# From the fourth feed-forward step on, both parts of the scaled tokens as one 512-column matmul operand

## What is computed

```python
h = h + merged @ w_out
hid = causal_dwconv(rms_norm(h, ffn_norm_g) @ w_ffn_up, ffn_conv_w, ffn_conv_b)   # width 3, 2*2816 channels
g_ff, up = jnp.split(hid, 2, axis=-1)
return h + (jax.nn.silu(g_ff) * up) @ w_ffn_down
# the whole is followed by a final RMSNorm
```

## Time and profile before

| | |
|---|---|
| median of 3 runs | 704.9 us (704.57 to 705.47) |
| the profiled execution, its own time | 704.42 us |
| its span, first to last instruction | 702.6 us |
| TensorE busy | 691.7 us, 98% of the span |
| VectorE busy | 493.6 us, 70% |
| ScalarE busy | 372.7 us, 53% |
| mean granted TensorE clock | 0.997 |

### The profile page before, as it was taken

The page is one execution under the profiler, slowest core; times in us unless marked ns, Lnnn a source line. Parts: engine busy times, 40 slices in busy tenths (PEclk is TensorE's granted clock), DMA queues, the critical chain, the costliest instruction groups (busy, mean ns, idle before and its releaser), DMA issues.

```text
span 702.6 us, 13155 instructions
## 1 busy us (share of the span) xinstructions
PE 691.7 (98%) x5210; PEld 657.5 (94%) x5210; DVE 493.6 (70%) x632; ACT 372.7 (53%) x472; POOL 9.7 (1%) x23
## 2 busy tenths in 40 slices
PE   9999999999999999999999999999999999999995
PEld 5999999999999999999999999999899999999994
DVE  5876989697876656667644456665568777777795
ACT  6539776767564554454533333333365555555552
POOL 0000000000100000000000000000000000000001
PEclk9999999999999999999999999999999999999998
DMA  8768576669536345345365755556626655555521
GB/s 236 226 204 278 167 248 178 229 191 355 156 109 190 122 153 180 120 142 159 121 188 182 257 186 156 185 177 222 213 75 206 198 179 179 179 186 188 198 87 60
DMA packets 112192, 127.60 MB, mean 182 GB/s; under 512 B 5358, under 2 KB 101151, under 8 KB 111647
## 3 DMA queue, kind: packets, MB, share of 16 engines
q1 hardware_dynamic: 112159, 127.14, 56.1%
HBM read 126.03 MB, written 2.67 MB: 183 GB/s over the span
## 4 chain that ended last, share of the span: by engine, by line
PE 88%; DVE 6%; ACT 2%; DMA 2%; issue 2%; SPq 0%; POOL 0%; DVEq 0%; POOLq 0%; ACTq 0%
PE ps L358 27%; PE ps L359 27%; PE ps L360 27%; DVE w_lo L330 2%; DVE conv_a L1311 1%; PE ps L400 1%; DMA acs_d<-acs_row 1%; PE ps L668 1%; DMA acs_b<-acs_d 1%; ACT decay L990 1%; PE ps L406 1%; PE ps L704 0%; PE ps L688 0%; DVE tok_lo L1216 0%; PE ps L653 0%
## 5 line engine op out<-in xcount | busy, mean ns | idle before, releaser
L358 PE MATMUL ps<-tok_hi,w_hi 128*128 128x256 f32 x1056 | 301.5, 285 | 1.1 <-DVE w_lo L1220 0.5
L359 PE MATMUL ps<-tok_lo,w_hi 128*128 128x256 f32 x1056 | 298.7, 283 | 0.0
L360 PE MATMUL ps<-tok_hi,w_lo 128*128 128x256 f32 x1056 | 298.7, 283 | 0.0
L330 DVE TENSOR_TENSOR w_lo<-w_raw,w_hi 128x2048 fp32r<-128x2048 f32 x108 | 247.0, 2288 | 67.0 <-ACT w_hi L326 67.0
L326 ACT ACTIVATE w_hi<-w_raw 128x2048 fp32r<-128x2048 f32 x108 | 206.2, 1910 | 57.4 <-PE ps L360 52.5
L358 PEld LDWEIGHTS ps<-tok_hi,w_hi 128*128 128x128 f32 x1056 | 202.4, 192 | 4.0 <-issue 2.0
L359 PEld LDWEIGHTS ps<-tok_lo,w_hi 128*128 128x128 f32 x1056 | 202.5, 192 | 0.4
L360 PEld LDWEIGHTS ps<-tok_hi,w_lo 128*128 128x128 f32 x1056 | 202.5, 192 | 0.0
L358 PE MATMUL ps<-os_hi,w_hi 128*128 128x256 f32 x128 | 36.3, 284 | 0.0
L360 PE MATMUL ps<-os_hi,w_lo 128*128 128x256 f32 x128 | 36.2, 283 | 0.0
L359 PE MATMUL ps<-os_lo,w_hi 128*128 128x256 f32 x128 | 36.2, 283 | 0.0
(11 more groups left out here) (280 smaller groups left out, 1063.8 us busy)
## 6 DMA issues: line engine op xcount, KB each, us to landing
w_raw<-w_in SPq DMA_DIRECT2D x94, 512.0 KB, 4.8
w_raw<-w_ffn_up SPq DMA_DIRECT2D x44, 512.0 KB, 4.4
w_raw<-w_ffn_down SPq DMA_DIRECT2D x22, 512.0 KB, 4.2
w_raw<-w_mem_kv SPq DMA_DIRECT2D x16, 512.0 KB, 4.4
w_raw<-w_br_ssm SPq DMA_DIRECT2D x16, 512.0 KB, 4.4
acs_b<-acs_d SPq DMA_DIRECT2D x4, 1024.0 KB, 6.6
w_raw<-w_br_attn SPq DMA_DIRECT2D x8, 512.0 KB, 4.4
w_raw<-w_br_mem SPq DMA_DIRECT2D x8, 512.0 KB, 4.0
```

Source lines behind the costliest of these rows:

```text
L330: dve.tensor_tensor(w_lo[:, s, :], w_raw[:, s, :], w_hi[:, s, :].bitcast(F32), ALU.subtract).then_inc(lo_ready[s], 1)
L358: pe.matmul(o, a[0], b[0], start=start, stop=False, **kw)
L359: pe.matmul(o, a[0], b[1], start=False, stop=False, **kw)
L360: return pe.matmul(o, a[1], b[0], start=False, stop=stop, **kw)
```

## The change

From step 3 on the up-projection takes other tokens. They are already scaled: h times gain times the token's factor, with high and low part side by side in one tile, `normed[:, k, 0, :]` and `normed[:, k, 1, :]`. The high part of the weights then meets both in one matmul of 512 columns, which fills a whole bank: the left half gets high times high, the right half high times low. The low part of the weights times the high tokens, 256 columns, is added to the right half. A product now fills two banks (a pair), one for each group of 128 output channels, and its result is the sum of a bank's halves. ScalarE copies the right halves of both banks into the pad (a new instruction that waits for the product), and VectorE adds the left halves to it and frees the pair.

The scaled tokens are made in steps 1 and 2, two quarters in each: VectorE adds the two token parts and multiplies by `rstd_b` (`normalise`), ScalarE makes the high part, VectorE the low part (`normalise_low`). These two steps are written out instead of looped. Some semaphores are merged as well (left out here); that changes no instruction's place.

```diff
+    def gemm_pair(pe, r, s, pair, freed):
+        pe.wait_ge(lo_ready[s], r + 2)
+        pe.wait_ge(bank_free[pair], freed)
+        for j in range(2):
+            b = 2 * pair + j
+            for k in range(KT):
+                w = slice(k * CW + j * P, k * CW + (j + 1) * P)
+                pe.matmul(ps[:, b, :], w_hi[:, s, w], normed[:, k, :, :].rearrange("p a t -> p (a t)"), start=k == 0,
+                          stop=False, skip_group_check=True)
+                mm = pe.matmul(ps[:, b, T:2 * T], w_lo[:, s, w], normed[:, k, 0, :], start=False, stop=k == KT - 1,
+                               skip_group_check=True)
+        mm.then_inc(gemm_done[s], 1)
...
-            with pe.Fori(1, F_STEPS - 2) as f:
+            for f in (1, 2):
                 r = f + (RG - 1)
                 gemm_cols(pe, r, 0, tok_hi, tok_lo)
                 gemm_cols(pe, r, 1, tok_hi, tok_lo)
                 down(r, 2, f, hid_hi, hid_lo)
...
+            with pe.Fori(3, F_STEPS - 2) as f:
+                r = f + (RG - 1)
+                gemm_pair(pe, r, 0, 0, r + 1)
+                gemm_pair(pe, r, 1, 1, r + 1)
+                down(r, 2, f, hid_hi, hid_lo)
+            gemm_pair(pe, RL - 1, 0, 0, RL)
+            gemm_pair(pe, RL - 1, 1, 1, RL)
+            gemm_pair(pe, RL - 1, 2, 0, RL + 1)
+            gemm_pair(pe, RL, 0, 1, RL + 1)
...
     (ScalarE, in ffn)
+                    if len(source) > 2:
+                        s, done = source[2:]
+                        act.wait_ge(gemm_done[s], done)
+                        act.wait_ge(f_step, 8 * f - 4 + 4 * n)
+                        act.activation(pad[:, :, FTAPS - 1:], ps[:, 2 * b:2 * b + 2, T:2 * T],
+                                       ACT.Copy).then_inc(crossed, 1)
...
+                    for q in norm if n == 0 else ():
+                        act.wait_ge(normed_t, 2 * q + 2)
+                        act.activation(normed[:, 2 * q:2 * q + 2, 0, :], norm_t[:, 2 * q:2 * q + 2, :],
+                                       ACT.Copy).then_inc(normed_hi, 1)
...
     (VectorE)
+            def normalise(q):
+                two = slice(2 * q, 2 * q + 2)
+                dve.tensor_tensor(norm_t[:, two, :], tok_hi[:, two, :].bitcast(F32), tok_lo[:, two, :].bitcast(F32),
+                                  ALU.add).then_inc(normed_t, 1)
+                dve.wait_ge(normed_t, 2 * q + 1)
+                dve.tensor_tensor(norm_t[:, two, :], norm_t[:, two, :], rstd_b[:].unsqueeze(1).to_broadcast([P, 2, T]),
+                                  ALU.mult).then_inc(normed_t, 1)
+            def normalise_low(q):
+                two = slice(2 * q, 2 * q + 2)
+                dve.wait_ge(normed_hi, q + 1)
+                dve.tensor_tensor(normed[:, two, 1, :], norm_t[:, two, :], normed[:, two, 0, :].bitcast(F32),
+                                  ALU.subtract).then_inc(normed_lo, 1)
...
+                    else:
+                        dve.wait_ge(crossed, 2 * f + n - 5)
+                        dve.tensor_tensor(inner, ps[:, 2 * b:2 * b + 2, 0:T], inner, ALU.add).then_inc(bank_free[b], 1)
```

More of the change, by code:

```diff
@@ L216, in build @@
     rstd_b = place("rstd_b", R + 18.5, [T])
+    normed = place("normed", R + 56, [KT, 2, T], F32R)
+    norm_t = place("norm_t", R + 72, [KT, T])
     pad_g = place("pad_g", R + 0, [2, FTAPS - 1 + T])
@@ L1147, in _, with ffn @@
             split_hi(act, RG, 0)
[L1150 to L1153, removed]
+            def ffn(f, gate, up, after_gate, after_up, last, first=False, hi=hid_hi, norm=()):
+                for n, (source, pad, conv, tile) in enumerate(((gate, pad_g, conv_g, 0), (up, pad_u, conv_u, FT))):
+                    b, freed = source[:2]
+                    if len(source) > 2:
[4 more added lines that the diff above has]
+                                       ACT.Copy).then_inc(crossed, 1)
+                    act.wait_ge(bank_free[b], freed)
                     if not first:
@@ L1171, in ffn @@
                     split_hi(act, rr, ss)
-            ffn(0, 1, RF + 3, 2, RF + 3, [(RG, 1)], [(RG, 2)], [], first=True)
-            with act.Fori(1, F_STEPS - 2) as f:
+            ffn(0, (1, RF + 3), (2, RF + 3), [(RG, 1)], [(RG, 2)], [], first=True)
+            for f in (1, 2):
                 r = f + (RG - 1)
-                ffn(f, 0, r + 2, 1, r + 2, [(r + 1, 0)], [(r + 1, 1)], [(r + 1, 2)])
-            ffn(F_STEPS - 2, 0, RL + 1, 1, RL + 1, [(RL, 0)], [(RL, 1)], [], hi=last_hi)
-            ffn(F_STEPS - 1, 2, RF + 4, 0, RL + 2, [(RL, 2)], [(RL + 1, 0)], [], hi=end_hi)
+                ffn(f, (0, r + 2), (1, r + 2), [(r + 1, 0)], [(r + 1, 1)], [(r + 1, 2)], norm=(2 * f - 2, 2 * f - 1))
+            with act.Fori(3, F_STEPS - 2) as f:
+                r = f + (RG - 1)
+                ffn(f, (0, r + 2, 0, r + 1), (1, r + 2, 1, r + 1), [(r + 1, 0)], [(r + 1, 1)], [(r + 1, 2)])
+            ffn(F_STEPS - 2, (0, RL + 1, 0, RL), (1, RL + 1, 1, RL), [(RL, 0)], [(RL, 1)], [], hi=last_hi)
+            ffn(F_STEPS - 1, (0, RL + 2, 2, RL), (1, RL + 2, 0, RL + 1), [(RL, 2)], [(RL + 1, 0)], [], hi=end_hi)
             for n in range(2 * NT):
@@ L1571, in _ @@
             dve.memset(pad_u[:, :, 0:FTAPS - 1], 0.0).then_inc(pads_zero, 1)
-            dve.wait_ge(x_again, 16)
+            dve.wait_ge(x_in[0], 32)
             split_lo(dve, RF + 1, 0)
@@ L1587, in _, with ffn, pad_with @@
             dve.wait_ge(pads_zero, 2)
[L1590 to L1595, removed]
+            def normalise(q):
[10 more added lines that the diff above has]
+                                  ALU.subtract).then_inc(normed_lo, 1)
+            def ffn(f, gate, up, early, after_gate, after_up, hi=hid_hi, lo=hid_lo, norm=()):
+                def pad_with(n, pad, splits):
+                    b, s, r = (gate, up)[n][:3]
+                    inner = pad[:, :, FTAPS - 1:]
+                    if len((gate, up)[n]) == 3:
+                        dve.wait_ge(gemm_done[s], r + 1)
+                        dve.tensor_tensor(inner, halves(s), rstd_b[:].unsqueeze(1).to_broadcast([P, 2, T]),
+                                          ALU.mult).then_inc(bank_free[s], 1)
+                    else:
+                        dve.wait_ge(crossed, 2 * f + n - 5)
+                        dve.tensor_tensor(inner, ps[:, 2 * b:2 * b + 2, 0:T], inner, ALU.add).then_inc(bank_free[b], 1)
                     for rr, ss in splits:
@@ L1609, in convolve @@
                                                      ALU.mult, ALU.add).then_inc(f_step, 1)
-                pad_with(sa, ra, pad_g, early)
+                for q in norm:
+                    normalise(q)
+                pad_with(0, pad_g, early)
                 convolve(0, pad_g, conv_g, 0)
-                pad_with(sb, rb, pad_u, [])
+                for q in norm:
+                    normalise_low(q)
+                pad_with(1, pad_u, [])
                 dve.wait_ge(g_tanh, f + 1)
@@ L1625, in ffn @@
                 dve.tensor_tensor(lo[:], hid[:], hi[:].bitcast(F32), ALU.subtract).then_inc(hid_lo_s, 1)
-            ffn(0, 1, RF + 1, 2, RF + 1, [(RG, 0)], [(RG, 1)], [])
-            with dve.Fori(1, F_STEPS - 2) as f:
+            ffn(0, (1, 1, RF + 1), (2, 2, RF + 1), [(RG, 0)], [(RG, 1)], [])
+            for f in (1, 2):
                 r = f + (RG - 1)
-                ffn(f, 0, r, 1, r, [(r, 2)], [(r + 1, 0)], [(r + 1, 1)])
-            ffn(F_STEPS - 2, 0, RL - 1, 1, RL - 1, [(RL - 1, 2)], [(RL, 0)], [(RL, 1)], last_hi, last_lo)
-            ffn(F_STEPS - 1, 2, RL - 1, 0, RL, [], [(RL, 2)], [(RL + 1, 0)], end_hi, end_lo)
+                ffn(f, (0, 0, r), (1, 1, r), [(r, 2)], [(r + 1, 0)], [(r + 1, 1)], norm=(2 * f - 2, 2 * f - 1))
+            with dve.Fori(3, F_STEPS - 2) as f:
+                r = f + (RG - 1)
+                ffn(f, (0, 0, r, "crossed"), (1, 1, r, "crossed"), [(r, 2)], [(r + 1, 0)], [(r + 1, 1)])
+            ffn(F_STEPS - 2, (0, 0, RL - 1, "crossed"), (1, 1, RL - 1, "crossed"), [(RL - 1, 2)], [(RL, 0)], [(RL, 1)],
+                last_hi, last_lo)
+            ffn(F_STEPS - 1, (0, 2, RL - 1, "crossed"), (1, 0, RL, "crossed"), [], [(RL, 2)], [(RL + 1, 0)], end_hi,
+                end_lo)
             def add_down(n):
@@ L1648, in scale_right @@
                                   ALU.mult).then_inc(y_right, 1)
-            dve.wait_ge(late_gain, 16)
+            dve.wait_ge(gain_in, 32)
             dve.wait_ge(h_sumsq, NT)
@@ L1660, in _, with rstd @@
         def _(pool):
-            def rstd(c, sumsq, var, done):
+            def rstd(c, sumsq, done):
                 for t in range(NT):
```

34 lines of the change are left out of this document (16 added, 18 removed).

## The result

The changed kernel takes 708.09 us (median of 5 runs, 707.36 to 709.00) against 704.9 of the kernel before (5 runs by now, 704.25 to 706.08): ratio 1.0044, 95% interval 1.0029 to 1.0058. It is slower by 3.2 us. That is inside the stated range of 704.0 to 708.8, but above the 706.1 of the forecast and outside the 705.2 to 707.2 of its likeliest case.

What follows compares the result with a forecast made beforehand. TensorE, busy for 98% of the span, was taken to bound the kernel. Pair -3.5, entry +3.3 and tail +1.4 make +1.2 us; on the median of 704.9 that gives 706.1 us, range 704.0 to 708.8.

Steps and rivals of the forecast that it cites:

- likeliest case: Whole execution: +1.2 us, 706.1 us, with a range of its own of 705.2 to 707.2; chance 0.67.
- The gaps at the entry: Steps 1 and 2: VectorE's scaling makes TensorE wait, 2.66 us ahead of down product 0, 3.3 us in all.
- Rival 2: Entry: the clock falls in the gap ahead of down product 0, costing 2.2 us, 708.3 us; chance 0.06.
- the second gap: Step 2: TensorE waits about 0.7 us ahead of gate product 2 for its late weight chunk.
- The gain of the pair: Steps 3 to 10: 0.0138 us less a slice over 256 slices, 3.5 us; bounds nothing and 10.2 us.
- The rule that was weighed: Steps 3 to 10: the skill's gap formula would save only 2.5 ns a slice, 0.6 us in all.
- Step 2 and the loop: Gate chunk of step 3 just fits, 16.7 against 16.98 us; steps 3 to 8 lose nothing, some 0.8 us left.
- Rivals 3 and 4: Loop: 3, late handoff in steps 3 to 8, 709.1 us, chance 0.06; 4, mixture hides fixed part, 702.6 us, 0.10.
- rival 1: Steps 3 to 10: the pair saves nothing, the mixture takes the three old distances, 709.6 us; chance 0.07.
- The tail: Step 10: the last up product's copy waits behind the tanh, so down product 9 starts 1.4 us late.
- the main case: The likeliest case: -3.5 pair, +3.3 entry, +1.4 tail, +1.2 us in sum; chance 0.67.
- two of its own signs: Prediction wrong if a loop step exceeds 16.7 us, or if the clock behind the entry gaps is below 1.

Runs made afterwards that it cites:

- x3: Changed kernel with twelve bf16 matmuls of 512 columns of zeros in the gap ahead of down product 0; 707.19 us.
- x6: Kernel before plus the scaling in steps 1 and 2, its scaled tokens not used, all products as before; 708.43 us.
- x4: Changed kernel with step 10's two up-projection products in the old form: three 256-column matmuls a slice, no copy by ScalarE; 707.41 us.
- x1: Changed kernel with the tokens scaled in steps 2 and 3 and the 512-column operand used from step 4 on; 704.66 us.
- x7: Changed kernel with two 512-column matmuls, then two 256-column ones, and so on in each bank; 706.38 us.
- x8: Changed kernel, 512- and 256-column matmuls still in turn, but the 256-column one takes the slice before; 707.74 us.
- x10: Changed kernel with VectorE's four scaling instructions in steps 1 and 2 behind the pad and down chunk's low part, not ahead; 710.07 us.

## Why the prediction was right or wrong

- **What bounds.** Right: TensorE sets the time in every step, and each change outside it counted only as a wait of TensorE.
- **The gaps at the entry.** Right in place, cause and size: 2.64 us against 2.66, and 0.6 against 0.67 where the clock holds (x3, x6).
- **The clock.** This step failed: "Against it: up to 698.0, as long as the new gap, it still shows 1.00". I read a clock that stays up while TensorE stands as one that stays up altogether. In the changed kernel it reads 1.00 in the gap as well and falls behind it. Rival 2 had a chance of 0.06 and came true, in five of the six profiled executions with this gap. Its price was too high: 2.2 us against 1.6, of which 0.6 only replaced the second gap, so 1.0 net.
- **The gain of the pair.** The mechanism was right, its term mis-sized: 0.0138 us a slice forecast, 0.0069 measured (0.3597, three of 0.1199, against 0.3528), and some 0.03 us more for each down product behind it. Two parts of the error: 0.2266 us for a long matmul came from the last 48, while in the loop a down product takes 5.47 us, 0.2279 each, which alone makes the saving 0.0119; the other 0.0050 is the cost of single turns, for which there was no row. The bounds were stated, and the value lay between them, half the way towards "saves nothing". (The upper bound was worked out wrongly, 256 x 0.0406 is 10.4 and not 10.2; nothing hung on it.)
- **The rule that was weighed.** An estimate from the gap formula of the Trainium skill ("TensorE: Matmul & The Clock Gate", section "Back-to-back issue gap") gave 0.6 us for the whole saving. The rows gave 3.5. Measured were 1.55, the table's two lines on products together, so the estimate was nearer. That was luck: its fixed part of 2.5 ns is not what these runs show (13.2 ns: 0.1199 us for 256 columns against 0.1067).
- **Step 2 and the loop.** Right: no gap ahead of gate product 3, none in steps 3 to 9. The loop's up pads stand 0.92 us behind their product (587.39 against 586.47), where about 1.0 was forecast. Rivals 3 and 4 fell; rival 1 is half true.
- **The tail.** Right in place and cause, shown by x4; 0.95 us against 1.4, since two products of 5.65 instead of 5.55 us gave VectorE 0.2 us more, and the last up pad came 0.84 instead of 0.98 us behind product 9.
- **The verdict.** "Just inside 0.2%" was the likeliest; the result is slower, 0.44%. What happened is a combination that the list didn't have, the main case with half clock and over half of rival 1: 1.2 + 0.9 (clock) + 2.0 (gain missed) - 0.45 (tail) + 0.1 = 3.8, the table's sum. That the time still lies in the stated range is partly luck: the range was made wide for other cases, and by two of its own signs the prediction was wrong, a loop step over 16.7 us (16.79) and a clock below 1 behind the gap (0.50).

## What to carry to other kernels

A wait that is put in front of the bounding engine costs its length and, when that engine is TensorE, perhaps the clock behind it as well, as here with 2.97 us from start to start; that the clock's row inside the gap still reads 1.00 doesn't rule it out. One-off work for a later gain belongs where the engine that does it has measured idle time (x1 against the changed kernel: 3.4 us for the same instructions one step later), and one step earlier it can cost more than the gain of all the steps. Where matmuls of two lengths are mixed, don't let them stand singly in turn; and where a short product is the last of a phase, its handoff chain decides, so leave the form with the shorter chain there.

## What was not expected of the hardware

- Behind the same gap of 2.97 us from start to start the granted clock fell at different moments: 0.2 us behind the end of the gap in the changed kernel, 1.2 us behind it in x7, and 0.4 us ahead of it in x8, still inside the gap. In x6 it didn't fall at all. Behind the 3.42 us of x10 it fell 1.2 us late, and behind 2.37 us (2.10 idle) near the start of x6 1.1 us late. So neither the length of a gap nor a clock that reads 1.00 when TensorE resumes tells what follows. Windows of x8, where TensorE resumes at 533.63, and of x7, where it resumes at 534.40:

```profile
533.00:534.00 1.00, 0.37 (x1) 0.40 (x2) 1.00 (x3) 1.00 (x1) 0.00 (x0) 0.63 0.00 0
```

```profile
535.00:536.00 1.00, 1.00 (x5) 0.83 (x4) 1.00 (x4) 1.00 (x3) 0.00 (x0) 0.81 0.41 74
```

- From the start of a 512-column matmul to the next start it took 0.2279 us among its own in the loop and 0.236 in single turns with 256-column ones, while the short one took 0.117 instead of 0.1199. Two by two both shift, to 0.233 and 0.115, but their sum is that of the grouped order: 0.348 us.
- The down product behind a product in single turns took 5.50 us instead of 5.47, its first matmuls standing 0.24 apart; behind the grouped ones it took 5.47. In x8, whose single turns end with two short matmuls, it took 5.46.
